# Storing the background projections to scratch DRAM: issued by ScalarE among its weight splits, where SyncE issued them among its weight loads

## The reference

```
h = x + 1/2 * SwiGLU_1(RMSNorm(x))
u = RMSNorm(h); P = u @ W_in            # one wide projection
A = RWKV-7 time mixing of P's first columns      (16 heads x 64)
B = gated DeltaNet of P's next columns           (8 value heads x 128, conv4, chunks of 64)
h = h + W_out( sigmoid(G_A) * (A @ L_A) + sigmoid(G_B) * (B @ L_B) )
h = h + CrossAttn_4heads(RMSNorm(h), RMSNorm(mem))
h = h + 1/2 * SwiGLU_2(RMSNorm(h))
y = RMSNorm_final(h)
```

## Time and profile before

| | |
|---|---|
| median of 3 runs | 2649.8 us (2646.39 to 2651.22) |
| the profiled execution's own time | 2646.74 us |
| its span, first to last instruction | 2644.8 us |
| granted TensorE clock | 0.998 |
| busy: PE, PEld, DVE, ACT, POOL | 99%, 82%, 59%, 46%, 7% |
| mean DMA rate | 207 GB/s |

### The profile page before, as it was taken

How to read it: one execution, slowest core, us unless ns; L and a number is a source line. 1 busy time by engine, 2 the same in 40 slices (tenths; PEclk the granted TensorE clock), 3 DMA queues, 4 the chain that set the end, 5 groups by cost and what they waited for, 6 DMA issues and landing times.

```text
span 2644.8 us, 35880 instructions
## 1 busy us (share of the span) xinstructions
PE 2620.9 (99%) x14101; PEld 2160.8 (82%) x14101; DVE 1561.7 (59%) x1802; ACT 1218.8 (46%) x1403; POOL 187.6 (7%) x344
## 2 busy tenths in 40 slices
PE   8999999999999999999999999999999999999998
PEld 7888888888888777888888888888888888888886
DVE  5555555555567796848566766555655555555444
ACT  5444444444456366446455544433544444444443
POOL 2000000000000011010001112000100000000000
PEclk9999999999999999999999999999999999999999
DMA  6767676766676575555488879644766767677664
GB/s 224 224 211 224 208 223 213 222 209 211 198 215 189 179 226 157 168 168 166 140 276 264 246 246 280 199 150 140 239 209 207 226 209 223 209 226 223 193 195 144
DMA packets 278440, 547.70 MB, mean 207 GB/s; under 512 B 24924, under 2 KB 35328, under 8 KB 277936
## 3 DMA queue, kind: packets, MB, share of 16 engines
q1 hardware_dynamic: 253856, 478.60, 58.1%
q0 software_dynamic: 24160, 66.89, 8.8%
q10 hardware_dynamic: 304, 0.53, 0.1%
HBM read 508.15 MB, written 37.77 MB: 206 GB/s over the span
## 4 chain that ended last, share of the span: by engine, by line
PE 93%; DVE 5%; ACT 2%; issue 1%; DMA 0%; SPq 0%; DVEq 0%; ACTq 0%
PE pp L328 29%; PE pp L330 29%; PE pp L329 29%; DVE wlo L289 1%; PE pa L2011 1%; PE pb L1996 1%; PE pa L986 0%; ACT whi L284 0%; ACT tmp L1646 0%; PE pb L986 0%; PE pa L1550 0%; DMA h<-in_x 0%; DVE inv_g L965 0%; PE pb L1550 0%; DVE s_g L1457 0%
## 5 line engine op out<-in xcount | busy, mean ns | idle before, releaser
L289 DVE TENSOR_TENSOR wlo<-raw,whi 128x1024 fp32r<-128x1024 f32 (+1 forms) x888 | 1078.6, 1218 | 917.9 <-ACT whi L284 910.8
L284 ACT ACTIVATE whi<-raw 128x1024 fp32r<-128x1024 f32 (+1 forms) x888 | 935.6, 1056 | 1292.5 <-PE pp L330 1244.8
L328 PE MATMUL pp<-whi,xhi 128*128 128x512 f32 (+1 forms) x2208 | 868.9, 394 | 0.7 <-DVE xlo L446 0.7
L329 PE MATMUL pp<-whi,xlo 128*128 128x512 f32 (+1 forms) x2208 | 857.7, 388 | 0.0
L330 PE MATMUL pp<-wlo,xhi 128*128 128x512 f32 (+1 forms) x2208 | 857.5, 388 | 0.0
L328 PEld LDWEIGHTS pp<-whi,xhi 128*128 128x128 f32 x2208 | 414.8, 188 | 93.3 <-issue 7.2
L330 PEld LDWEIGHTS pp<-wlo,xhi 128*128 128x128 f32 x2208 | 415.0, 188 | 86.0
L329 PEld LDWEIGHTS pp<-whi,xlo 128*128 128x128 f32 x2208 | 415.2, 188 | 82.1
L328 PE MATMUL pp<-whi,hhi 128*128 128x512 f32 x704 | 273.9, 389 | 0.0
L329 PE MATMUL pp<-whi,hlo 128*128 128x512 f32 x704 | 273.9, 389 | 0.0
L330 PE MATMUL pp<-wlo,hhi 128*128 128x512 f32 x704 | 273.9, 389 | 0.0
(11 more groups left out here) (433 smaller groups left out, 2036.0 us busy)
## 6 DMA issues: line engine op xcount, KB each, us to landing
raw<-in_ffn_w_gate SPq DMA_DIRECT2D x176, 512.0 KB, 4.3
raw<-in_ffn_w_up SPq DMA_DIRECT2D x176, 512.0 KB, 4.5
raw<-in_ffn_w_down SPq DMA_DIRECT2D x176, 512.0 KB, 3.9
raw<-in_w_in SPq DMA_DIRECT2D x144, 512.0 KB, 4.3
hid_dram<-hid_t POOLq DMA_DIRECT2D x43, 512.0 KB, 3.3
xq<-hid_dram POOLq DMA_DIRECT2D x156, 128.0 KB, 4.8
raw<-in_w_lift SPq DMA_DIRECT2D x32, 512.0 KB, 5.7
raw<-in_w_out SPq DMA_DIRECT2D x32, 512.0 KB, 5.0
```

Of the source, the lines that this page charges most:

```text
L284: nc.scalar.activation(whi[:, s, :, 0:width], raw[:, s, :, 0:width], ACT.Copy).then_inc(whi_ready, 1)
L289: nc.vector.tensor_tensor(wlo[:, s, :, 0:width], raw[:, s, :, 0:width], whi[:, s, :, 0:width].bitcast(F32), ALU.subtract).then_inc(wlo_rea ...
L328: nc.tensor.matmul(out, a_hi[:, k0 + k, tok], w_hi, start=first, stop=False)
L329: nc.tensor.matmul(out, a_lo[:, k0 + k, tok], w_hi, start=False, stop=False)
```

## The change

SP issues loads only. ACT issues the stores: for a turned projection behind its split of the eighth slot (j == 7), after a wait for DVE's transposition; for the others right behind its own copy. The three tables are changed at 40 names (11 of `STEPS`, 12 of `SLOTS_ACT`, 17 of `SLOTS_DVE`); four of them are shown.

```diff
         def load_slot(sp, src, base_slot, j, i=0, width=CW):
...
             sp.dma_start(dst, src).then_inc(LOADED[s], 16)
-            if isinstance(n, int) and n in STORE_BEHIND:
-                spool_store(sp, STORE_BEHIND[n])
...
         def bg_act(act, name):
...
                 if j == 4 and q > 0:
                     spool_out(act, q - 1)
+                if j == 7 and q > 0 and q - 1 in TURNED:
+                    spool_store(act, q - 1)
...
         def spool_out(act, q):
...
             scaled_copy(act, spool_of(q), pr["par"]).then_inc(sem(pr["released"][0]), 1)
+            act.wait_ge(sem(pr["released"][0]), pr["released"][1])
+            act.dma_start(proj[q].rearrange("(t p) c -> p t c", p=P), spool_of(q)[:, :, :]).then_inc(sem("spooled"), 16)
...
-        STORE_BEHIND = {BG[q + 1]["slot"] + (11 if q in TURNED else 9): q for q in range(len(BG) - 1)}
-        STORE_BEHIND[prods["lift"][0]["slot"] + 6] = len(BG) - 1
-
-        def spool_store(sp, q):
-            pr = BG[q]
-            if q in TURNED:
-                sp.wait_ge(sem("spool_turned"), TURNED.index(q) + 1)
-                sp.dma_start(turned_proj(q), spool_blocks(q)).then_inc(sem("spooled"), 16)
-            else:
-                sp.wait_ge(sem(pr["released"][0]), pr["released"][1])
-                sp.dma_start(proj[q].rearrange("(t p) c -> p t c", p=P), spool_of(q)[:, :, :]).then_inc(sem("spooled"), 16)
+        def spool_store(act, q):
+            act.wait_ge(sem("spool_turned"), TURNED.index(q) + 1)
+            act.dma_start(turned_proj(q), spool_blocks(q)).then_inc(sem("spooled"), 16)
...
 STEPS = {
-    "gdn0.y": 14,
+    "gdn0.y": 12,
...
-    "inv1.rows": 11, "inv1.10": 1, "inv1.20": 1, "inv1.30": 1, "inv1.40": 1,
+    "inv1.rows": 11, "inv1.10": 3, "inv1.20": 1, "inv1.30": 1, "inv1.40": 1,
...
-    "rw0.lora": 4, "rw0.g": 10, "rw0.kk": 7, "rw0.tilde": 10, "rw0.nat": 1, "rw0.mats0": 3, "rw0.mats1": 3,
+    "rw0.lora": 4, "rw0.g": 11, "rw0.kk": 6, "rw0.tilde": 10, "rw0.nat": 1, "rw0.mats0": 3, "rw0.mats1": 3,
```

## The result

The changed kernel takes 2654.5 us in the median of 20 runs (2650.9 to 2660.7), the kernel before 2647.6 us (2645.3 to 2651.2): a ratio of 1.0026, 95% interval 1.002 to 1.0033, so 0.26% or 6.8 us slower. The profiled executions are 2654.87 us (span 2653.1) and 2646.74 us (span 2644.8), 8.1 us apart. The time lies inside my range of 2646.5 to 2655, but by luck: I had laid the range around a median of 2649.8 us for the kernel before, which these runs put at 2647.6, and moved by that difference its upper edge would be 2652.8. I forecast +1.5 us, and the size of the loss is what has to be explained.

What follows compares the result with a forecast made beforehand. PE bounds the kernel, busy for 2620.9 of 2644.8 us. The terms gdn1 1.2, rw0 0.5 and rw1 -0.2 sum to +1.5 us on a median of 2649.8, so 2651 us; range 2646.5 to 2655.

Steps and rivals of the forecast that it cites:

- Store q = 0 ... Cost 0: First moved store: ACT stands 6.4 us for the transposition, DVE takes the split with 1.2 us to spare; cost 0.
- Rival 4: Background stretch: half of the 17 stores each delay a split by 2.5 us, PE loses 7 us, 2657 us; chance 0.05.
- Rival 3: Eight turned stores: ACT stuck at transpositions, four pass on about 1.5 us each, +6 us, 2656 us; chance 0.10.
- the 3.5 us at q = 4: Sign at the store of q = 4, in gdn1's inversion: ACT's wait for the transposition is 3 to 5 us.
- gdn1: Ahead of its inversion 0.7 us, in it waits of 0.7 and 0.3 where 0.5 was; together 1.2 us.
- without the two extra steps it would be 2.7 us more: gdn1's inversion: without the two steps added ahead of the second block multiply, the cost would be 2.7 us more.
- rw0: At L1517 0.1 us of new wait for `gs`, ahead of L1523 0.4 us from one step fewer; 0.5 in the sum.
- rw1: `rw1.g`'s two extra steps about match ACT's added work; only the 0.2 us wait on `inv_s` goes: -0.2 us.
- The gates' stores: Straight behind ACT's own copy: 2.9 us in a slot of 2.715, made good in the next; cost 0.
- the 0.4 to 0.5 that I had named as a sign: Sign in the changed kernel's profile: ACT issues 17 stores at 0.4 to 0.5 us each, SP none.

Runs made afterwards that it cites:

- e3: The changed kernel with the store of projection 0 issued by SyncE behind its load 11, as before, the other 16 by ScalarE: 2651.9 us, ratio 1.0012.
- e12: The changed kernel with GpSimd's fetches of projection 0 held until ScalarE's split of slot 315, the store staying early: 2650.9 us, ratio 1.0014.
- e5: The kernel before with SyncE issuing the store of projection 0 one load earlier, behind load 10: 2650.8 us, ratio 1.0010.
- e6: The changed kernel with ScalarE issuing the store of projection 0 later, behind split 2 of the next projection but one: 2652.5 us, ratio 1.0016.
- e4: The changed kernel with the eight turned stores issued by ScalarE one slot later: 2655.6 us, ratio 1.0023.
- e1: The changed kernel with the three tables of the kernel before, stores still on ScalarE: 2653.8 us, ratio 1.0021.
- e2: The changed kernel's new tables with the stores left on SyncE as in the kernel before: 2648.9 us, ratio 1.0004.
- e8: The changed kernel with SyncE's first store, plus two background steps more ahead of rw1's identity products and two fewer behind its last chunk: 2650.1 us, ratio 1.0011.
- e10: The kernel before with one of the 10 background steps ahead of rw1's identity products moved behind them: 2651.9 us, ratio 1.0015.
- e9: The changed kernel with GpSimd's fetches held until TensorE has used 311 slots, a hold that proved empty: 2654.3 us, ratio 1.0028.
- e11: The kernel before with two background steps ahead of rw1's identity products moved behind them: 2654.0 us, ratio 1.0024.

## Why the prediction was off in size

- **"Store q = 0 ... Cost 0"** is the step that failed. Its arithmetic for ACT and DVE was right: 6.93 us of idle time against 6.4 + 0.47, and PE's waits there don't name the transposition. What was wrong is the sentence ahead of it: "POOL's fetches move with it, and no wait of PE names them." PE does not wait for the fetches, but a weight load is late beside them, ACT's split waits for the load, ACT's copy for the split, and PE for the copy. Measured: 2.7 us in the trace, 2.9 (e3) and 3.1 (e12) on the median, each against the kernel before in its own runs. Shown by e3, e5, e6 and e12.
- **Rival 4** (the loads suffer) is the right family, and I gave it 0.05. Its place was wrong: I had half of the 17 stores delay the splits a little; the one store tried early without its fetches costs PE no wait (e12). It is the burst of six fetches behind one of them, at one copy without cover.
- **Rival 3** (ACT stuck at the transpositions) did not happen. ACT's other long stops at stores were the 3.5 us at q = 4 that I expected (3 to 5), 3.3 around the store at 1080.67 and 4.2 around that at 1117.63; e4, with 3.3 us in all, was no faster.
- **gdn1:** 0.7 us forecast ahead of the inversion, 0.8 measured. In the inversion I forecast a wait of 0.7 us at the second multiply and 0.3 in place of 0.5 at the third; neither came, and the old 0.50 us is gone. The prediction's "without the two extra steps it would be 2.7 us more" is e1's 2.3 us.
- **rw0:** the 0.1 us at L1517 (line 1511) didn't come, the 0.4 at L1523 did (0.36 in the marks of the two traces).
- **rw1** I had put at -0.2: in the changed kernel it costs 1.8 us for the LoRA piece, 2.0 of wait and 1.6 of half clock at the identity products, and the 0.2 on `inv_s` is still there. e2 shows that the two waits, 1.4 and 1.5 us of them, come with the tables alone. I had balanced ACT's longer list against `rw1.g`'s two steps, but not looked at where these came from (`rw1.kk`) nor at a load that lands late there too (ACT's split waits 3.1 us for it at 1231.4, 1.9 in the kernel before; 3.0 to 3.2 in e2, e3, e8 and e12). The wait there goes the way of gdn0's: late load, ACT's split, VectorE's, PE.
- **The gates' stores** and the ACT issues: no wait of PE names them, as forecast. An issue takes ACT 0.33 to 0.43 us, less than the 0.47 taken over from SyncE and mostly less than the 0.4 to 0.5 that I had named as a sign.

By the medians the sum is: tables 1.0 us (e2 over before, not distinguishable from 0), the other 16 stores 3.0 (e3 over e2), first store 2.9 (changed over e3, each against the kernel before of its own runs), together the 6.8. Of the 3.0 us the two traces show 2.1 at the identity products (0.7 more wait in e3 than in e2, 1.4 of clock) and some 0.2 us at each of four places between gdn1 and the end of rw0. What the 16 stores do there no run shows (the split ahead waits for its load as long in e2, 3.16 us, as in e3, 3.23), and the fall of the clock is in part luck, since e12 waited nearly as long without it. The intervals of the ratios leave each term uncertain by some 2 us.

What stays open: whether the fetches slow a load by their bytes alone. The six are 1.5 MB, at the 386 GB/s of a busy stretch an estimated 4 us of all DMA engines, about what the load lost (9.0 us against 4.7). But none of the runs changed their size or form. No kernel tried beats the kernel before.

## What to carry to other kernels

A store that moves takes with it every transfer that waits for its landing. Price that burst against the loads on whose hour it falls, and follow the late load through its consumer's list to the instruction that stands behind it; the issuer's own time was the small part here. If the burst hits a load without cover, holding the burst by one wait was worth as much here as moving the store back (1.0014 and 1.0012). And where PE waits some 2 us ahead of many small products, book the wait and, as a risk, products at half clock behind it: a step given to one wait is best taken from a place whose slack has been read off the trace.

## What the runs showed of the hardware

TensorE's granted clock fell to 0.50 behind short stops between small products. At the identity products it stayed at 1.00 behind waits of 0.96 us (e5) and 1.46 (e2), and fell behind 1.98 (changed), 2.12 (e3 and e4), 2.21 (e10), 2.34 (e9), 3.16 (e6) and 3.45 us (e11); but in e12 the same wait of 1.98 us left it at 1.00, with products of 2.08 and 2.06 us. At gdn0's inversion it fell behind 2.05 (e5), 2.49 (e9), 2.56 (e4) and 3.06 us (e1), and in the changed kernel a wait of 2.69 us left it alone. The Trainium skill (TensorE: Matmul & The Clock Gate, section "Part 1: The HAM clock gate") knows just these two levels and says that the moment of a transition varies from run to run; the rows agree with both. So the same wait has two prices. Single runs of one kernel lie some microseconds apart, and this may be one reason, though no run here separates it from others.
